# Token norms in two halves of 64 columns, and a new order in the last chunk of the state space stage

## The chip, the cores and the metric

The kernel runs on one core of a Trainium2 chip. The metric is the device time of one execution in microseconds (us), the median of the runs shown. A core has five engines that run their own instruction streams and wait for each other by semaphores: TensorE (PE, its weight loads are listed as PEld), VectorE (DVE), ScalarE (ACT), GpSimd (POOL) and SyncE (SP, which here only issues DMAs).

## The reference

Two transformer-like blocks over one sequence of 512 tokens with 1024 features, all in float32. Before and after each mixer stands an RMS norm over the features of a token:

```
def rms_norm(x, g):
    y = xf * lax.rsqrt(jnp.mean(xf * xf, axis=-1, keepdims=True) + EPS)
    return (y * g.astype(jnp.float32)).astype(x.dtype)

h = rms_norm(x, mix_pre_g) * (1.0 + sc1) + sh1
x = x + g1 * rms_norm(hybrid_mixer(h, ...), mix_post_g)      # attention and convolution
h = rms_norm(x, ffn_pre_g) * (1.0 + sc2) + sh2
x = x + g2 * rms_norm(swiglu_ffn(h, ...), ffn_post_g)
# second block
h = modulate(x, norm_g[0], shift, scale)
x = x + gate * mamba2_mixer(h, ...)                          # chunked state space, 4 chunks of 128 tokens
k, v = modulate(x, kv_norm_g, ...) @ kv_w
x = x + gate * sb_mixer(modulate(x, norm_g[1], ...), k, v, ...)   # stick-breaking attention
return rmsnorm(x, final_g)
```

At the end of the mamba2 mixer the output `y` is gated and normalised in 4 groups of 512 features, and then projected:

```
y = y.reshape(b, s, M_D_INNER) * jax.nn.silu(z)
yg = y.reshape(b, s, M_GROUPS, M_D_INNER // M_GROUPS)
yg = yg * lax.rsqrt(jnp.mean(yg * yg, axis=-1, keepdims=True) + EPS)
y = yg.reshape(b, s, M_D_INNER) * norm_g
return y @ out_w
```

## The kernel before

Features lie on the 128 partitions and tokens in the columns, so an activation is 8 tiles of 128x512. A float32 product is made from three passes: each operand is split into a high part and a rest (`whi` and `wlo` for weights, `hhi` and `hlo` for activations). Weights come in panels of 1 MB; ACT copies the high part of one (`split_hi`), DVE subtracts it (`split_lo`), and PE may use panel c only when `lo_split` has counted c + 1. There are two buffers, so a panel's split waits until the panel before its buffer has been used, and its DMA until the split of that one.

A norm over the features of a token is a sum over partitions. ACT squares a tile, and PE sums it with a matmul against ones (`token_sums`, one quarter of the tokens on each 32 partitions, so that all 512 sums lie in 128 columns). When all eight tiles are in, three steps follow each other, each on another engine: ACT takes the square root (`token_std`, 128x128), DVE the reciprocal in place (`token_rs`), and PE copies each quarter's row to all partitions by four float32 matmuls with a broadcast column of the identity as the weights (`spread`). Only then can DVE scale the tiles (L419 in a post-norm, L457 in a pre-norm, L2366 at the end), ACT makes the high part (L466), and PE starts the next product (L478). This chain is run seven times: once at the head of the kernel, twice after the attention (post-norm and the following pre-norm), twice after the FFN, once after the state space stage (its spread is the last thing before a block boundary, at which all engines meet) and once at the end.

`post_norm(..., late=(41, 54, sums, parts))` also places 13 small modulation products (`columns`, L382: 2 matmuls each, one column wide with 128x128 weights) on PE: `parts[0]` of them between the last sums and the first spread, `parts[1]` behind the first spread, `parts[2]` and `parts[3]` among the second sums, `parts[4]` ahead of the second spread, and `parts[5]` behind it.

In the state space stage every chunk has 8 batches of 4 heads. For each, ACT makes decays (L1726 to L1732), DVE masks them (`masked`, L1849 and L1854), and PE multiplies (L1578, L1581). The last chunk also gates the 4 groups on DVE (`gate_part`, L1379), squares them on ACT (`group_squares`, L1705), sums them on PE (`squares`, L1515), and takes root (`group_std`, L1716), reciprocal (`group_rs`, L1383), spread (`group_spread`, L1523) and the scaled low and high parts (`norm_lo`, L1388 and L1395; `hi_part`, L1407). The product with the output weights (`m_panel`, L1635) has eight panels; panel k of the first half needs group k. All orders are written out by hand: each engine runs its list in the order of the code, and nothing reorders it.

## Time and profile before

| | |
|---|---|
| time, median of 3 runs | 1412.69 us (1410.79 to 1412.97) |
| the profiled execution's own time | 1412.92 us |
| its span, first to last instruction | 1411.1 us |
| mean granted TensorE clock | 0.976 |
| busy: PE, DVE, ACT, POOL | 96%, 58%, 42%, 29% |

The busy shares are means over stages with different limits. The times below are in us from the start of the span, and all views are of this one execution. A matmul in float32 shows as two passes in the trace, each with its own weight load, so the 4 matmuls of a spread are 8 records.

### The profile page before, as it was taken

How to read it: one execution, taken by the hardware profiler on the slowest of the kernel's cores; microseconds unless marked ns; L12 is line 12 of the kernel's file. 1: busy time of each engine (PE TensorE's matmuls, PEld its weight loads, DVE VectorE, ACT ScalarE, POOL GpSimd, SP SyncE). 2: the span in 40 equal slices, each digit the busy share in tenths (PEclk: the TensorE clock that was granted, in tenths of full speed). 3: DMA queues.
4: the chain of work that ended last, by engine and by line, in shares of the span. 5: the costliest groups of instructions: out<-in, count | busy, mean ns of one | idle time of the engine just before them, and what ended most of it. 6: DMA issues, size and time to landing. Idle time of an engine off the chain costs nothing. (4 is left out here: it accounts for less than half of the span.)

```text
span 1411.1 us, 19533 instructions
## 1 busy us (share of the span) xinstructions
PE 1348.2 (96%) x7904; PEld 1072.8 (76%) x7904; DVE 823.5 (58%) x965; ACT 588.5 (42%) x849; POOL 407.2 (29%) x191
## 2 busy tenths in 40 slices
PE   5999999799999999999999999999998999999996
PEld 3778867578888888887788876767776899777775
DVE  2789974566555564433757656778733822566544
ACT  4323656332222232113444456787522422455441
POOL 0000000149887888998100000000000050232310
PEclk9999999889999999999799999999999999999998
DMA  9434071124545536543222243334132432111121
GB/s 382 156 136 150 31 268 61 60 90 178 186 171 223 189 128 235 209 178 149 93 91 89 92 131 93 113 119 143 60 111 91 156 121 90 60 60 34 57 90 60
DMA packets 41350, 181.12 MB, mean 128 GB/s; under 512 B 3392, under 2 KB 20160, under 8 KB 21312
## 3 DMA queue, kind: packets, MB, share of 16 engines
q1 hardware_dynamic: 40128, 171.73, 33.9%
q10 hardware_dynamic: 1152, 8.39, 1.7%
q8 instruction: 51, 0.84, 0.2%
q14 instruction: 19, 0.16, 0.0%
HBM read 173.75 MB, written 6.36 MB: 128 GB/s over the span
## 5 line engine op out<-in xcount | busy, mean ns | idle before, releaser
L193 DVE TENSOR_TENSOR wlo<-raw,whi 128x2048 fp32r<-128x2048 f32 x95 | 257.4, 2710 | 169.2 <-ACT whi L189 166.6
L200 POOL TENSOR_TENSOR ada_raw<-ada_raw,cs 128x2048 f32<-128x2048 f32 x36 | 142.6, 3962 | 498.6 <-DVE h2lo L451 451.0
L271 PE MATMUL ps<-hhi,whi 128*128 128x512 f32 x640 | 252.1, 394 | 2.3 <-PEq L563 0.8
L271 PE MATMUL ps<-hhi,wlo 128*128 128x512 f32 x640 | 249.4, 390 | 0.0
L271 PE MATMUL ps<-hlo,whi 128*128 128x512 f32 x640 | 249.1, 389 | 0.0
L189 ACT ACTIVATE whi<-raw 128x2048 fp32r<-128x2048 f32 x95 | 181.5, 1911 | 143.6 <-PE ps L1312 91.3
L209 POOL TENSOR_TENSOR ada_raw<-ada_raw 128x1024 f32<-128x1024 f32 x72 | 166.0, 2305 | 5.6
L271 PEld LDWEIGHTS ps<-hhi,whi 128*128 128x128 f32 x640 | 120.2, 188 | 28.6 <-issue 2.4
L271 PEld LDWEIGHTS ps<-hhi,wlo 128*128 128x128 f32 x640 | 120.1, 188 | 25.6
L271 PEld LDWEIGHTS ps<-hlo,whi 128*128 128x128 f32 x640 | 120.3, 188 | 24.3
L2041 POOL TENSOR_TENSOR x<-x,rest 128x256 f32<-128x256 f32 (+3 forms) x32 | 49.0, 1532 | 160.2 <-DVE rest L2340 160.2
L2340 DVE TENSOR_TENSOR_SCAN rest<-rest,zero 128x128 f32<-128x128 f32 (+3 forms) x64 | 59.0, 962 | 59.0 <-ACT rest L2257 59.0
L1262 ACT ACTIVATE fg<-ps 128x512 f32<-128x512 f32 x22 | 13.2, 599 | 174.4 <-PE ps L271 174.4
L739 DVE SCALAR_TENSOR_TENSOR cv<-u,vec,cv 128x512 f32<-128x512 f32 x120 | 81.9, 743 | 0.4
L1810 DVE SCALAR_TENSOR_TENSOR xbc<-ps,vec,xbc 128x511 f32 (+5 forms) x72 | 48.4, 741 | 41.9 <-ACT xbc L1666 41.8
L1277 DVE TENSOR_TENSOR fg<-ps,fg 128x512 f32<-128x512 f32 x22 | 15.2, 691 | 98.4 <-ACT fg L1262 98.4
L1312 PE MATMUL ps<-flo,whi 128*128 (+1 forms) x176 | 70.2, 399 | 0.0
L433 POOL TENSOR_TENSOR x<-x,y 128x512 f32<-128x512 f32 x4 | 5.1, 1270 | 225.0 <-DVE y L419 225.0
L1312 PE MATMUL ps<-fhi,whi 128*128 (+1 forms) x176 | 69.7, 396 | 0.0
L1312 PE MATMUL ps<-fhi,wlo 128*128 (+1 forms) x176 | 69.0, 392 | 0.0
L1503 PE MATMUL ps<-hhi,whi 128*128 128x512 f32 x128 | 55.3, 432 | 0.5 <-DVE wlo L193 0.5
L1503 PE MATMUL ps<-hlo,whi 128*128 128x512 f32 x128 | 50.3, 393 | 0.0
(374 smaller groups left out, 2781.1 us busy)
## 6 DMA issues: line engine op xcount, KB each, us to landing
raw<-panels SPq DMA_DIRECT2D x87, 1024.0 KB, 4.9
ada_raw<-ada SPq DMA_DIRECT2D x48, 1024.0 KB, 6.7
first<-ada SPq DMA_DIRECT2D x8, 1024.0 KB, 20.6
bc<-ac_rows SPq DMA_DIRECT2D x32, 256.0 KB, 3.7
raw<-panels ACTq DMA_DIRECT2D x8, 1024.0 KB, 5.0
x_kept<-x SPq DMA_DIRECT2D x2, 2048.0 KB, 9.7
x<-x_kept SPq DMA_DIRECT2D x2, 2048.0 KB, 7.7
x<-x_in SPq DMA_DIRECT2D x1, 2048.0 KB, 10.8
```

Of the source, the lines that this page charges most:

```text
L189: e.activation(whi[:, c % 2, :, :], raw[:, c % 2, :, :], ACT.Copy).then_inc(hi_split, 1)
L193: e.tensor_tensor(wlo[:, c % 2, :, :], raw[:, c % 2, :, :], whi[:, c % 2, :, :].bitcast(F32), ALU.subtract).then_inc(lo_split, 1)
L200: e.tensor_tensor(ada_raw[:, c % 2, :, :], ada_raw[:, c % 2, :, :], cs[:, which, :].unsqueeze(2).to_broadcast([P, KT, 256]), ALU.mult).the ...
L209: e.tensor_tensor((ada_acc[:, c % 2, :] if sums is None else sums).unsqueeze(1) if width == 1 else part, part, ada_raw[:, c % 2, width:2 * ...
L271: mm = e.matmul(ps[:, 2 * (qc % 2) + b, :], w[:, c % 2, 2 * k + b, :], src[part][:, k, :], **flags)
L739: dve.scalar_tensor_tensor(out=cv[:, j, :], in0=src, scalar=w, in1=cv[:, j, :], op0=ALU.mult, op1=ALU.add).then_inc(A["tap"], 1)
L1277: dve.tensor_tensor(fg[:, pair, :], ps[:, 2 * pair + 1, :], fg[:, pair, :], ALU.mult).then_inc(prod_ready, 1)
L1312: mm = pe.matmul(ps[:, b, :], w[:, c % 2, k2 * 8 + b, :], src[:, kt, :] if isinstance(i, int) else src[:, bass.ds(kt + i * 4, 1), :], star ...
L1503: mm = pe.matmul(ps[:, 2 * (qp % 2) + b, :], wt[:, cp % 2, 2 * kt + b, :], (hhi, hlo)[part][:, kt, :], start=(kt == 0 and j == 0), stop=(k ...
L1810: ins = dve.scalar_tensor_tensor(out=xbc[:, bass.ds(t, 1), s:S], in0=ps[:, 2 * pair + b, 0:S - s], scalar=vec[:, bass.ds(wc, 1)], in1=xbc[ ...
L2041: pool.tensor_tensor(sig[:, n % 3, :, 0:nk], sig[:, n % 3, :, 0:nk], rest[:, n % 2, :, S - nk + 1:S + 1], ALU.mult).then_inc(B["am"], 1)
L2340: scan = dve.tensor_tensor_scan(turned, turned, zero[:, 0:1].to_broadcast([P, nk]), 1.0, ALU.mult, ALU.add)
```

## The change

The square root, the reciprocal and the spread of the token norms work on 64 columns at a time (`TOKEN_HALVES`): two instructions on ACT, two on DVE, eight matmuls on PE instead of four. Each engine can start on a half when the engine ahead has finished that half; PE also waits for both square roots, since it overwrites the bank that they read. The norm of the groups in the state space stage is not split.

The small modulation products after the FFN move: `parts` goes from `[3, 3, 1, 1, 2, 3]` to `[4, 5, 1, 1, 2, 0]`.

In the last chunk of the state space stage the gate of group 0 comes behind the masks of batch 4 on DVE instead of ahead of them; on ACT the squares of group 3 come ahead of the high parts of group 2; the split of the fourth output panel (`cm + 3`) comes ahead of the scaled parts of group 3 on both engines. The coefficients of the two pre-norms of the last block are computed at the end of the block before.

```
         def token_std(act, no, s, bank):
             act.wait_ge(*no("ss_used", (s + 1) * KT))
-            act.activation(rsq[:], ps[:, bank, 0:P], ACT.Sqrt, bias=eps[:, 0:1],
-                           scale=1.0 / D).then_inc(nsem["std_ready"], 1)
+            for h in TOKEN_HALVES:
+                act.activation(rsq[:, h], ps[:, bank, h], ACT.Sqrt, bias=eps[:, 0:1],
+                               scale=1.0 / D).then_inc(nsem["std_ready"], 1)

         def token_rs(dve, no, s):
-            dve.wait_ge(*no("std_ready", s + 1))
-            dve.reciprocal(rsq[:], rsq[:]).then_inc(nsem["rs_ready"], 1)
+            for i, h in enumerate(TOKEN_HALVES):
+                dve.wait_ge(*no("std_ready", 2 * s + i + 1))
+                dve.reciprocal(rsq[:, h], rsq[:, h]).then_inc(nsem["rs_ready"], 1)

         def spread(pe, no, s, bank):
-            pe.wait_ge(*no("rs_ready", s + 1))
-            for b in range(TB):
-                mm = pe.matmul(ps[:, bank, b * P:(b + 1) * P], ident[:, 32 * b:32 * b + 1].to_broadcast([P, P]), rsq[:],
-                               start=True, stop=True)
+            pe.wait_ge(*no("std_ready", 2 * s + 2))
+            for i, h in enumerate(TOKEN_HALVES):
+                pe.wait_ge(*no("rs_ready", 2 * s + i + 1))
+                for b in range(TB):
+                    mm = pe.matmul(ps[:, bank, b * P + h.start:b * P + h.stop],
+                                   ident[:, 32 * b:32 * b + 1].to_broadcast([P, P]), rsq[:, h], start=True, stop=True)
             mm.then_inc(nsem["spread"], 1)
...
-                post2 = post_norm(..., late=(41, 54, sums, [3, 3, 1, 1, 2, 3]))
+                post2 = post_norm(..., late=(41, 54, sums, [4, 5, 1, 1, 2, 0]))
...                                                     # ACT, end of the state space stage
-                        hi_part(act, 2)
                         group_squares(3)
+                        hi_part(act, 2)
                         split_hi(act, cm + 2, 0)
                         group_std(3)
+                        split_hi(act, cm + 3, 0)
                         hi_part(act, 3)
                         act.activation(warm[:, 5:6], ones[:, 0:1], ACT.Sqrt)
-                        for k in range(1, MT // 2 - 1):
+                        for k in range(2, MT // 2 - 1):
...                                                     # DVE, last chunk
                                     if g < MG - 1 and not (c == TB - 1 and b == 1):
                                         masked(n + 2)
+                                        if c == TB - 1 and g == 1:
+                                            gate(0)
+                                            masked(n + 3)
...
-                                    if g < MG - 1:
+                                    if g in (0, 2):
                                         masked(c * NB + 2 * g + 3)
...
+                                    if g > 0:
+                                        gate(g)
...
                         norm_lo(dve, 2)
                         split_lo(dve, cm + 2, 0)
                         group_rs(dve, 3)
+                        split_lo(dve, cm + 3, 0)
                         norm_lo(dve, 3)
+                        norm_coefs(dve, v("kv_norm"), "kvsc", 1)
+                        norm_coefs(dve, v("norm2", KT, KT), "ssc", 2)
...                                                     # DVE, last block
-                    pre3["coefs"](dve)
-                    pre4["coefs"](dve)
                     pre3["dve"](dve)
```

On PE, behind the FFN: from the last sums of the post-norm (L316) over both spreads (`ps<-rsq`) to the first product of the next stage (L478). `macc` and `fg` hold the sums that the small modulation products read. First before, then after the change:

```order
L316 MATMUL ps<-y_place,consts 32x128 x12
L382 MATMUL ps<-consts,macc 128x1 x6
L336 MATMUL ps<-rsq,consts 128x128 x4
L382 MATMUL ps<-consts,macc 128x1 x6
L316 MATMUL ps<-y_place,consts 32x128 x12
L382 MATMUL ps<-consts,macc 128x1 x2
L316 MATMUL ps<-y_place,consts 32x128 x12
L382 MATMUL ps<-consts,macc 128x1 x2
L316 MATMUL ps<-y_place,consts 32x128 x8
L382 MATMUL ps<-consts,macc 128x1 x2
L382 MATMUL ps<-consts,fg 128x1 x2
L336 MATMUL ps<-rsq,consts 128x128 x4
```

```order
L317 MATMUL ps<-y_place,consts 32x128 x12
L387 MATMUL ps<-consts,macc 128x1 x8
L341 MATMUL ps<-rsq,consts 128x64 x8
L387 MATMUL ps<-consts,macc 128x1 x10
L317 MATMUL ps<-y_place,consts 32x128 x12
L387 MATMUL ps<-consts,fg 128x1 x2
L317 MATMUL ps<-y_place,consts 32x128 x12
L387 MATMUL ps<-consts,fg 128x1 x2
L317 MATMUL ps<-y_place,consts 32x128 x8
L387 MATMUL ps<-consts,fg 128x1 x4
L341 MATMUL ps<-rsq,consts 128x64 x8
L486 MATMUL ps<-hhi,whi 128x512
```

Two of the small matmuls moved ahead of the first spread and four more stand behind it; the six that stood behind the second spread are gone from there, and both spreads have twice the matmuls, each with weights of its own.

On ACT, in the last chunk, from the root of group 2 (`state<-ps`) to the split of the weight panels (`whi<-raw`). `ada_raw<-xbc` are the squares, `y2hi<-xbc` the high parts, `zb` the gate's silu. Before and after:

```order
L1716 ACTIVATE state<-ps,eps 128x128
L1698 ACT_TABLE_LOAD
L1698 ACTIVATE zb<-zb 128x1024 x2
L175 DMA raw<-panels 128x2048
L1407 ACTIVATE y2hi<-xbc 128x512 x4
L1705 ACTIVATE ada_raw<-xbc 128x512 x4
L189 ACTIVATE whi<-raw 128x2048
L1716 ACT_TABLE_LOAD
L1716 ACTIVATE state<-ps,eps 128x128
L1407 ACTIVATE y2hi<-xbc 128x512 x4
```

```order
L1706 ACTIVATE zb<-zb 128x1024 x2
L175 DMA raw<-panels 128x2048
L1713 ACTIVATE ada_raw<-xbc 128x512 x4
L1415 ACTIVATE y2hi<-xbc 128x512 x4
L189 ACTIVATE whi<-raw 128x2048
L1724 ACT_TABLE_LOAD
L1724 ACTIVATE state<-ps,eps 128x128
L189 ACTIVATE whi<-raw 128x2048
L1415 ACTIVATE y2hi<-xbc 128x512 x4
```

The four squares of group 3 now stand ahead of the four high parts of group 2, and the split of the third panel (`cm + 2`) stands where it stood, behind both; the split of the fourth panel moved ahead of the high parts of group 3.

On DVE, in the last chunk, from the skip terms of group 0 (`xbc<-xbc,vec,ps 128x128 x4`) over the masks (`dec`, `ce`) and the gate (`xbc<-xbc,x`) to the skip terms of group 1. Before and after:

```order
L1900 SCALAR_TENSOR_TENSOR xbc<-xbc,vec,ps 128x128 x4
L1849 TENSOR_TENSOR dec<-dec,cb 128x512
L1854 TENSOR_TENSOR ce<-ce,xbc 128x512
L1379 TENSOR_TENSOR xbc<-xbc,x 128x2048
L1849 TENSOR_TENSOR dec<-dec,cb 128x512
L1854 TENSOR_TENSOR ce<-ce,xbc 128x512
L1900 SCALAR_TENSOR_TENSOR xbc<-xbc,vec,ps 128x128 x4
```

```order
L1917 SCALAR_TENSOR_TENSOR xbc<-xbc,vec,ps 128x128 x4
L1858 TENSOR_TENSOR dec<-dec,cb 128x512
L1863 TENSOR_TENSOR ce<-ce,xbc 128x512
L1858 TENSOR_TENSOR dec<-dec,cb 128x512
L1863 TENSOR_TENSOR ce<-ce,xbc 128x512
L1387 TENSOR_TENSOR xbc<-xbc,x 128x2048
L1858 TENSOR_TENSOR dec<-dec,cb 128x512
L1863 TENSOR_TENSOR ce<-ce,xbc 128x512
L1917 SCALAR_TENSOR_TENSOR xbc<-xbc,vec,ps 128x128 x4
```

The gate of group 0 moved behind one more pair of masks, and the pair that followed the skip terms of group 1 now stands ahead of them.

## Rows read from the trace of the kernel before

**Rows 1.** The page: busy us (share) and instructions of each engine.

```profile
PE 1348.2 (96%) x7904; PEld 1072.8 (76%) x7904; DVE 823.5 (58%) x965; ACT 588.5 (42%) x849; POOL 407.2 (29%) x191
```

**Rows 2.** Timeline (start us, us, engine, line) of the norms after the attention.

```profile
268.50 0.37 ACT L324 ACTIVATE rsq<-ps,eps 128x128 f32<-128x128 f32 x1 [0.55 <-PE ps L316]
...
269.91 1.19 PEld L336 LDWEIGHTS ps<-rsq,consts 128*128 128x128 f32 x8 [1.74 <-DVE rsq L330]
...
282.69 1.78 PEld L336 LDWEIGHTS ps<-rsq,consts 128*128 128x128 f32 x8 [1.93 <-DVE rsq L330]
```

**Rows 3.** Two lines' own views: durations in ns (least/median/most).

```profile
L330 DVE RECIPROCAL rsq<-rsq x7: 952/953/953, 18.6 to 1399.4; 128x128 f32<-128x128 f32 x7
```

```profile
L1165 DVE RECIPROCAL rinv<-rsum x16: 148/154/165, 131.8 to 215.5; 128x2 f32<-128x2 f32 x16
```

**Rows 4.** Timeline of the norms after the FFN.

```profile
665.80 1.42 PEld L382 LDWEIGHTS ps<-consts,macc 128*128 128x128 f32 x12 [0.20 <-issue]
...
667.35 0.97 PEld L336 LDWEIGHTS ps<-rsq,consts 128*128 128x128 f32 x8
...
679.95 1.83 PEld L336 LDWEIGHTS ps<-rsq,consts 128*128 128x128 f32 x8
...
681.66 2.68 PEld L382 LDWEIGHTS ps<-consts,fg 128*128 128x128 f32 x12
...
682.89 1.38 ACT L466 ACTIVATE hhi<-y_place,mod 128x512 fp32r<-128x512 f32 x2 [4.10 <-DVE y_place L457]
...
684.28 0.77 PE L478 MATMUL ps<-hhi,whi 128*128 128x512 f32 x1
```

**Rows 5.** Stretches of PE: us, PE busy (passes), granted clock, DMA share, GB/s.

```profile
286.40:291.00 4.60, 4.55 (x11) 0.50 0.00 0
...
684.30:690.40 6.10, 6.10 (x15) 0.50 0.00 0
...
1085.60:1089.70 4.10, 1.48 (x19) 1.00 0.00 0
...
1092.00:1096.60 4.60, 4.59 (x11) 0.50 1.01 426
...
1400.40:1403.00 2.60, 2.06 (x8) 0.50 0.00 0
```

**Rows 6.** Timeline of the head and of the last block boundary.

```profile
19.57 0.97 PEld L336 LDWEIGHTS ps<-rsq,consts 128*128 128x128 f32 x8 [0.53 <-DVE rsq L330]
...
1090.15 0.24 DVE L443 SCALAR_TENSOR_TENSOR coef<-mod,vec 128x8 f32<-128x8 f32 x2 [1.54 <-PEq L1449]
```

**Rows 7.** Timeline of the last chunk, gate of group 0 to panel 0.

```profile
967.75 0.68 DVE L1849 TENSOR_TENSOR dec<-dec,cb 128x512 f32<-128x512 f32 x1
...
969.13 0.45 PE L1578 MATMUL ps<-dec,ada_raw 128*64 128x128 f32 x4 [0.94 <-DVE dec L1849]
...
982.75 0.47 PE L1635 MATMUL ps<-hhi,whi 128*128 128x512 f32 x1 [0.28 <-DVE hlo L1395]
```

**Rows 8.** Timeline of the last chunk behind the gate of group 3, by engine.

```profile
1007.29 2.17 ACT L1705 ACTIVATE ada_raw<-xbc 128x512 f32<-128x512 f32 x4
1009.37 1.89 ACT L189 ACTIVATE whi<-raw 128x2048 fp32r<-128x2048 f32 x1
...
1002.67 1.40 DVE L1388 SCALAR_TENSOR_TENSOR xbc<-xbc,vec,ps 128x512 f32<-128x512 f32 x2
...
1011.29 2.29 DVE L193 TENSOR_TENSOR wlo<-raw,whi 128x2048 fp32r<-128x2048 f32 x1 [3.19 <-ACT whi L189]
...
1008.01 0.23 PEld L1515 LDWEIGHTS ps<-ada_raw,consts 128*32 128x32 f32 x8 [3.29 <-issue]
...
1013.64 0.19 PEld L1635 LDWEIGHTS ps<-y2hi,whi 128*128 128x128 f32 x1 [0.40 <-DVE wlo L193]
...
1026.71 0.50 PE L1635 MATMUL ps<-y2hi,whi 128*128 128x512 f32 x1 [0.69 <-DVE wlo L193]
```

**Rows 9.** PE behind that wait: us, PE busy (passes), clock, DMA.

```profile
1008.00:1010.00 2.00, 1.96 (x32) 0.50 0.03 8
```

More of the change, by code:

```diff
@@ L342, in post_norm @@
             N = nsem
-            no = counting(bank_done=KT - 1, kept=KT, sq_ready=2 * KT, ss_used=2 * KT, std_ready=2, rs_ready=2, spread=2,
+            no = counting(bank_done=KT - 1, kept=KT, sq_ready=2 * KT, ss_used=2 * KT, std_ready=4, rs_ready=4, spread=2,
                           scaled=KT, x_new0=KT // 2, x_new1=KT // 2, coef_ready=1)
@@ L435, in post_norm, with norm_coefs @@
             return dict(pe=on_pe, act=on_act, coefs=coefs, mods=mods, dve=on_dve, pool=on_pool)
+        def norm_coefs(dve, gain, sc, slot, k0=0, k1=KT):
+            dve.scalar_tensor_tensor(out=coef[:, slot, k0:k1], in0=m(sc)[:, k0:k1], scalar=1.0, in1=gain[:, k0:k1],
+                                     op0=ALU.add, op1=ALU.mult).then_inc(nsem["coef_ready"], 1)
         def pre_norm(gain, sc, sh, thi, tlo, h0, rs, slot=1, parts=1):
@@ L442, in coefs @@
             def coefs(dve, k0=0, k1=KT):
-                dve.scalar_tensor_tensor(out=coef[:, slot, k0:k1], in0=m(sc)[:, k0:k1], scalar=1.0, in1=gain[:, k0:k1],
-                                         op0=ALU.add, op1=ALU.mult).then_inc(N["coef_ready"], 1)
+                norm_coefs(dve, gain, sc, slot, k0, k1)
             def on_dve(dve, k0=0, k1=KT):
@@ L558, in build @@
             x_landed = sem("x_landed")
-            x0 = counting(sq_ready=KT, ss_used=KT, std_ready=1, rs_ready=1, spread=1)
+            x0 = counting(sq_ready=KT, ss_used=KT, std_ready=2, rs_ready=2, spread=1)
             head = pre_norm(v("mix_pre"), "sc1", "sh1", hhi, hlo, h0, ps[:, 7, :], parts=4)
@@ L1226, in build @@
                 last = co + COUNT["ffn_out"] - 1
-                post2 = post_norm("ffn_post", "g2", y_place[:, 0:KT, :], y_place[:, 8:11, :], last, late=(41, 54, sums, [3, 3, 1, 1, 2, 3]))
+                post2 = post_norm("ffn_post", "g2", y_place[:, 0:KT, :], y_place[:, 8:11, :], last, late=(41, 54, sums, [4, 5, 1, 1, 2, 0]))
                 pre2 = pre_norm(v("norm2", 0, KT), "msc", "msh", hhi, hlo, y_place[:, 11:13, :],
@@ L1440, in build @@
                 xsq = dec[:, 0:2, :, :].rearrange("p a h t -> p a (h t)")
-                no = counting(bank_done=3, x_new1=KT, sq_ready=KT, ss_used=KT, std_ready=1, rs_ready=1, spread=1)
+                no = counting(bank_done=3, x_new1=KT, sq_ready=KT, ss_used=KT, std_ready=2, rs_ready=2, spread=1)
                 M = {k: sem("m_" + k) for k in ("cols", "cols_c", "wend0", "ends", "xdt", "xw", "bt", "btok",
@@ L1856, in masked, with gate @@
                                                   .to_broadcast([P, HB, P]), ALU.mult).then_inc(M["ce"], 1)
+                        def gate(g):
+                            dve.wait_ge(M["yskip"], 4 * (TB - 1) * MG + 4 * g + 4)
+                            dve.wait_ge(G["z"], 2 * g + 2)
+                            gate_part(dve, g)
                         for c in range(TB):
@@ L1954, in x_step @@
                                                      op1=ALU.add).then_inc(nsem["x_new1"], 1)
-                        for k in range(1, MT // 2 - 1):
+                        for k in range(2, MT // 2 - 1):
                             split_lo(dve, cm + k + 2, 0)
@@ L1987, in build @@
             pre4 = pre_norm(v("norm2", KT, KT), "ssc", "ssh", h2hi, h2lo, h0, ps[:, 7, :], slot=2)
-            fin = counting(bank_done=KT - 1, x_new1=KT, sq_ready=KT, ss_used=KT, std_ready=1, rs_ready=1, spread=1,
+            fin = counting(bank_done=KT - 1, x_new1=KT, sq_ready=KT, ss_used=KT, std_ready=2, rs_ready=2, spread=1,
                            out_ready=KT, out_stored=16 * KT)
```

6 lines of the change are left out of this document (2 added, 4 removed).

## The prediction, made before the changed kernel had run

> **What bounds the kernel now.** I read the page first: PE is busy for 96% of the span, so only what PE waits for, or what PE itself does more of, moves the time [rows 1]. The timelines of the places that the diff touches come next, since the mean hides them. Two kinds stand out. One is the token norm: root on ACT, reciprocal on DVE, spread on PE, with nothing else for PE to do. From the start of the root at 268.50 to the first weight load of the spread at 269.91 pass 1.41 us; the spread's loads then take 1.19 us there and 1.78 us at 282.69 [rows 2]. The other is the last chunk of the state space stage, where PE waits 0.94 us for a mask at 969.13 [rows 7], 3.29 us for the squares of group 3, and 0.69 us at 1026.71 for `wlo` [rows 8]. The split makes the 1.41 us shorter; the new order aims at the waits. So I ask what each pays.
>
> **What a half costs.** One reciprocal of 128 columns takes 953 ns, one of 2 columns 154 ns [rows 3]. On the line between them 64 columns take 0.54 us; I take that, bounds 0.48 (half) and 0.95. The root takes 0.37 us for 128 columns [rows 2]; no row has a shorter one of these, so I take 0.30, bounds 0.19 and 0.37. The first half then reaches PE after 0.30 + 0.54 and the two hand-overs of today (1.41 - 0.37 - 0.95 = 0.09), at 0.93 us instead of 1.41: 0.48 us earlier. The second half is ready at about 1.4 us, while PE still works on the first, so it costs no wait.
>
> PE pays for it. A spread goes from 4 matmuls to 8, from 8 passes to 16, each with its own load of 128x128 weights. What is a pass of 64 columns? The spread's 8 loads of 128 columns span 0.97 us at 667.35; the small modulation products, one column wide with the same weights, span 1.42 us for 12 at 665.80 [rows 4]. Without the last load's own 0.19 that is 0.111 and 0.112 us for a pass. At the half clock it is (1.83 - 0.33) / 7 = 0.214 and (2.68 - 0.33) / 11 = 0.214 [rows 4]. A pass of 128 columns and one of 1 column cost the same: the weight load sets it, and 64 columns lie between. So the eight more passes cost 0.89 us at the full clock (2.4 GHz), 1.71 us at half (1.2 GHz). Less the 0.48 won, a chain becomes **0.41 us longer at full, 1.23 us at half**. Bounds of one chain: -0.5 us if a pass of 64 columns cost half of one of 128, and +1.7 us if the start came no earlier.
>
> The Trainium skill ("TensorE: Matmul & The Clock Gate", section on the back-to-back issue gap) gives a gap by moving columns, N / 2.4 + 2.5 ns when warm, by which a pass of 64 would be the cheaper; its own LDWEIGHTS section counts the 128 columns of the weights instead. By the first rule the chains would give -2.7 us in place of the +5.7 below (rival C); the rows above bear out the second.
>
> **The seven chains, one by one.**
> Head: PE idles 0.53 us ahead of its spread [rows 6], so it can start early, but then issues 16 passes; +0.4 to +0.6. What follows (modulation, tiles, split of the first panel, next modulation) runs back to back over DVE, and PE goes on from it. Part of it lies at the half clock either way. +0.4, bounds 0 and +0.6.
> After the attention: the first spread starts at full and slows down in its last loads, 1.19 against 0.97 us [rows 2, 4]. With 16 passes more of them fall there: 0.41 and four to five passes 0.1 us slower, +0.8. The second is at half: +1.23.
> After the FFN, first: four small products now stand ahead, 16 passes or 1.78 us from 665.80, so the spread starts at 667.58 instead of 667.35; the early half is of no use. +0.23 and +0.89 = +1.12. Second: two products stand ahead as before and end when the reciprocal does, so nothing is won, +1.71. But six matmuls are gone behind it: today they keep PE until 684.28, while the high part is there at 682.89 + 0.72 (half of the pair's 1.38, rounded up) = 683.6. This gives 0.55 back: +1.16. The six matmuls put behind the first spread take 4 products more, 0.9 to 1.7 us, while PE waits for squares; covered. Uncovered it would be +1.
> Behind the state space stage: full clock until 1089.7 [rows 5], +0.41, and the two `coef` instructions at 1090.15 leave the path, 0.24 us for both and 0.21 to the next start [rows 6]: +0.2. At their new place DVE waits for panels.
> End: at the half clock from 1400.40 [rows 5]; the early half of a us has some passes at full. +0.8, bounds +0.4 and +1.23.
> Sum: 0.4 + 0.8 + 1.23 + 1.12 + 1.16 + 0.2 + 0.8 = **+5.7 us**.
>
> **The last chunk.** The mask of batch 4 waits behind the gate of group 0, until 967.75; with the gate behind it PE's 0.94 us at 969.13 goes. But that gate starts two steps of about 0.6 us (the mask rows, 0.68 each) later, and ACT squares group 0 only behind it, with the decays of the last two batches and the root of group 0 queued after the squares. Root, reciprocal and spread come later by about 1.3 us, where DVE had some 1 us in hand; panel 0, which already waits for `hlo` at 982.75 [rows 7], starts 0 to 0.3 us later. I take +0.15 for the edit: the stall moves, it does not go.
>
> The squares of group 3: their gate ends where DVE takes up the scaled parts, 1002.67. ACT can square from about 1003.0 to 1005.1 (2.17 us) instead of from 1007.29, and PE finds them ready: its 3.29 us wait goes. What is late next? The high parts of group 2 start at 1005.1 instead of 1003.4, so DVE's low parts end at 1009.7 instead of 1008.1, and the split of panel `cm + 2`, still behind both, starts at 1008.9 on ACT instead of 1009.37. DVE then splits at 1010.8 instead of 1011.29 [rows 8]. PE needs just this: at 1013.64 it starts the panel, released by `wlo`, after 0.40 us without a load [rows 8]. So PE, through with its old work at 1009.1, now waits there until 1013.2, for 4.1 us, and **wins only 0.45 us of 3.3**. The early split of `cm + 3` takes the 0.69 us at 1026.71, with the run-out of the last pass 0.9. Together -1.35.
>
> Today, behind the 3.29 us without work, PE runs at 0.50 [rows 9]; the work in that stretch is hidden, since PE meets `wlo` anyway. In the new order the wait is longer and what follows is not hidden: some 3 us of products at half the clock cost 1.5 us (bounds 0 and 2.2). Without the slow clock it is -1.2 for this part; with it, it is -1.35 + 0.15 + 1.5 = **+0.3 us**.
>
> **Sum.** 5.7 + 0.3 = 6.0, against the profiled execution's own 1412.92 us (span 1411.1 and 1.8 around it; it lies 0.23 above the median of 1412.69): **1418.7 us**, taken as a median 0.2 down from 1418.9. That is 0.4% slower.
>
> **Rivals.** What can be told from no change is about 0.2%, 2.8 us; so "faster" begins below 1409.9 and "slower" above 1415.5.
> A, the forecast: weight loads set the pass. 0.58; its own range 1416 to 1421.5.
> B, the order in the last chunk pays in full, since the split of `cm + 2` comes in time or the clock stays up: 3.3 and 0.9 and up to 0.4 us of the stretched squares, -4.6. For it: the waits are in the rows. Against it: ACT does the same work ahead of that split. 5.7 - 4.6 on 1412.9 is 1414. 0.16.
> C, the moving columns set the pass: a split spread is as long as before and starts 0.48 earlier. Then after the attention -1.0, after the FFN +0.2 and -0.55, boundary -0.7, end -0.5, head -0.2: -2.7, with +0.3 it is 1410.5. Against it: one column costs what 128 do. 0.07, about half of it with part of B, below 1409.9. The Trainium skill's rule of the issue gap (page above) would have it so.
> D, on the other side: the clock. The products behind the norms run at 0.50 for 4.60, 6.10 and 4.60 us [rows 5], half of this lost, 7.6 us, and the spreads there lose 0.8 each. If twice the loads keep PE at full through these stretches, 7.6 and some 2.5 us come back: 6.0 - 10.1, 1408.8. It decides from two of the three stretches. Against it: PE moves no more columns than before, and 36 small passes did not keep it up after the FFN. 0.05.
> E, the longer chains make the half-clock stretches longer: three to seven us more at half cost 1.5 to 3.5 us: 1420.2 to 1422.2. 0.14.
>
> **Range and chances.** 1412.5 to 1421.5: it leaves out C, D and about half of E. Slower: A's part above 1415.5 (0.55) and E, 0.69. Same: B, the rest of A and half of C, 0.22. Faster: D and the other half of C, 0.09.
>
> **What would show it.** Right: 16 loads of a spread spanning 1.85 us at full and 3.5 at half; two reciprocals of 0.54 us; the first load 0.93 us after the root's start (not after the FFN, where small products stand ahead); PE released by `wlo` at the start of panel `cm + 2` after about 4 us, and no wait before `cm + 3`; the first product after the FFN 2.3 us later from 665.80. Wrong: loads of 64 columns less than 0.1 us apart; panel `cm + 2` starting straight behind the squares of group 3; the granted clock at 1.00 in the pre-norms' first products.

## The result, and the profile after

The changed kernel takes 1423.67 us (median of 5, 1421.5 to 1425.69) beside 1412.97 us for the kernel before (median of 5, 1410.79 to 1414.84): a ratio of 1.0068, 95% interval 1.0053 to 1.0082. The ratio is not the quotient of the two medians: by it the loss is 9.6 us, by the medians 10.7. It is slower, as predicted, but by about 10 us and not by 6, and it lies above my range (1412.5 to 1421.5). Two later sets gave 1.0067 [1.0043, 1.0091] and 1.0076 [1.0059, 1.0093]. The profiled execution took 1425.69 us, with a span of 1423.5 us and a mean granted clock of 0.969 against 0.976.

The page of the changed kernel, busy us and instructions, answers to [rows 1]:

```profile
PE 1361.0 (96%) x7960; PEld 1086.6 (76%) x7960; DVE 821.6 (58%) x972; ACT 589.1 (41%) x856; POOL 405.2 (28%) x191
```

56 passes more (7 chains of 8), and PE is busy for 12.8 us more. By 0.112 and 0.213 us a pass (below) these are 6.3 us at the full clock and 11.9 if each were at the half clock, which few are: so more of the other work must have run slower too.

The timeline of the two norms after the attention, answers to [rows 2]:

```profile
272.24 0.52 ACT L326 ACTIVATE rsq<-ps,eps 128x64 f32<-128x64 f32 x2 [0.55 <-PE ps L317]
272.59 0.96 DVE L333 RECIPROCAL rsq<-rsq 128x64 f32<-128x64 f32 x2
...
273.26 2.58 PEld L341 LDWEIGHTS ps<-rsq,consts 128*128 128x128 f32 x16 [1.35 <-ACT rsq L326]
...
285.92 0.52 ACT L326 ACTIVATE rsq<-ps,eps 128x64 f32<-128x64 f32 x2 [0.78 <-PE ps L317]
...
286.93 3.49 PEld L341 LDWEIGHTS ps<-rsq,consts 128*128 128x128 f32 x16 [1.54 <-ACT rsq L326]
```

The first load now comes 1.02 us (272.24 to 273.26) after the root's start instead of 1.41. But sixteen loads take 2.58 and 3.49 us instead of 1.19 and 1.78. The two lines' own views, answering to [rows 3]:

```profile
L333 DVE RECIPROCAL rsq<-rsq x14: 494/524/554, 16.9 to 1410.9; 128x64 f32<-128x64 f32 x14
```

```profile
L326 ACT ACTIVATE rsq<-ps,eps x14: 297/308/313, 16.6 to 1410.3; 128x64 f32<-128x64 f32 x14
```

The timeline behind the FFN, answering to [rows 4], gives the price of a pass most plainly, since two kinds stand in a row:

```profile
672.26 1.86 PEld L387 LDWEIGHTS ps<-consts,macc 128*128 128x128 f32 x16 [0.20 <-issue]
...
674.04 1.87 PEld L341 LDWEIGHTS ps<-rsq,consts 128*128 128x128 f32 x16
...
687.48 3.53 PEld L341 LDWEIGHTS ps<-rsq,consts 128*128 128x128 f32 x16
```

Sixteen passes of one column took 1.86 us, sixteen of 64 columns 1.87 us. Less the last load's own 0.19 that is 0.112 us a pass either way, and (3.53 - 0.33) / 15 = 0.213 at the half clock.

Last, stretches of PE: us, PE, PEld, DVE, ACT and POOL busy, granted clock, DMA share, GB/s; they answer to [rows 5] and [rows 9]:

```profile
195.80:202.60 6.80, 6.80 (x36) 5.03 (x36) 3.05 (x7) 3.90 (x10) 0.00 (x0) 0.50 0.51 173
288.00:298.00 10.00, 8.31 (x27) 6.95 (x27) 7.08 (x11) 3.55 (x5) 0.00 (x0) 0.50 0.21 89
...
946.80:950.00 3.20, 3.20 (x18) 2.00 (x15) 2.81 (x9) 3.17 (x3) 0.00 (x0) 0.50 0.12 35
1022.70:1028.60 5.90, 5.86 (x15) 4.71 (x16) 3.14 (x2) 1.14 (x1) 0.00 (x0) 0.50 0.72 221
```

Two of these are new, 195.8 to 202.6 and 946.8 to 950.0, and they lie in the attention and in the state space stage, where the diff touches nothing. Two others are longer: PE is at 1.2 GHz until 298 (before: until 291.0, which is 294.7 with the 3.74 us that these norms start later), and behind the wait in the last chunk until 1028.6. Not all of this is lasting: r_after, a second profile of the same kernel, has the stretch in the attention stage, but not the one at 947, and the two others are no longer than before.

How late the changed kernel is, stage by stage. Each number is the median, over DVE's instructions that both traces have in that stretch of the kernel before (3 to 223 of them), of start now minus start before; the last is the difference of the spans:

| place (us of before) | profile of the result | 2nd profile (r_after) | 3rd profile (r2_after) | my sum up to there |
|---|---|---|---|---|
| behind the head (60 to 120) | -0.4 | +1.5 | +1.4 | +0.4 |
| attention stage, late (205 to 265) | +3.8 | +5.8 | +6.1 | +0.4 |
| behind the attention's norms (300 to 640) | +6.5 | +6.9 | +8.8 | +2.4 |
| behind the FFN's norms (700 to 930) | +8.0 | +8.0 | +10.3 | +4.7 |
| before the last chunk (951 to 965) | +9.6 | +8.0 | +11.9 | +4.7 |
| behind the last chunk (1045 to 1075) | +10.8 | +7.9 | +13.1 | +5.0 |
| last block (1110 to 1380) | +11.1 | +9.7 | +13.4 | +5.2 |
| end | +12.4 | +10.7 | +14.6 | +6.0 |

One line is out in all three: between 185 and 205 us the kernel loses 4.1 to 4.7 us where I had nothing. (An unchanged copy of the kernel before lies 1.8 us behind its first profile after the head, so differences of 2 us there are scatter.)

### The profile page after: what moved, and what is told of

It reads as the page before. It is cut to its first block and busy times, and to the rows that moved or that the text cites. A ratio compares the mean times of both kernels' runs of the same rounds, so it can differ in the third digit from the quotient of the medians.

```text
span 1423.5 us, 19666 instructions
## 1 busy us (share of the span) xinstructions
PE 1361.0 (96%) x7960; PEld 1086.6 (76%) x7960; DVE 821.6 (58%) x972; ACT 589.1 (41%) x856; POOL 405.2 (28%) x191
## 5 line engine op out<-in xcount | busy, mean ns | idle before, releaser
L1270 ACT ACTIVATE fg<-ps 128x512 f32<-128x512 f32 x22 | 13.2, 599 | 174.1 <-PE ps L271 174.1
```

## The experiments

Each kernel ran beside the kernel before on the same chip; ratios are to it. The sets differ by up to 4 us in what the kernel before takes (1412.97 to 1417.13), so I compare ratios, and a loss or gain in us is the ratio on that set's median. There is one profile of each kernel and set, of one execution.

### The halves, and the rest

e1_halves is the kernel before with the new `token_std`, `token_rs` and `spread` and nothing else; e2_rest is the changed kernel with these three as before.

```
-            for h in TOKEN_HALVES:                                    # e2_rest
-                act.activation(rsq[:, h], ps[:, bank, h], ACT.Sqrt, ...)
+            act.activation(rsq[:], ps[:, bank, 0:P], ACT.Sqrt, ...)
```

> The kernel before with the split token norms alone (root, reciprocal and spread in two halves of 64 columns), nothing else of the change. Theory 1, each pass of the spread is set by its weight load (0.111 us at the full clock, 0.214 at half): head +0.4 to +1, after the attention +0.9 and +1.2, after the FFN +0.7 and +1.7, boundary +0.4, end +1.2: +6 to +7.5 us. Rival C, moving columns set the pass: -3 us. Rival D, the added passes keep the clock up: -2 or less, and no stretch at 0.50 behind the norms.

> The changed kernel with the token norms whole again: only the order in the last chunk, the places of the small products and the coefficients. Theory 1: small products -0.3, coefficients -0.2, last chunk between -1.2 (clock stays up behind the new wait for wlo) and +1.5 (it falls to half for some 5 us): -1.7 to +1.0 us in all. If the order of the last chunk were worth what its waits show (rival B), -4.5 or less. If most of what the changed kernel lost beyond the forecast is in this part, +3 or more.

Measured: e1_halves 1422.61, ratio 1.0050 [1.0034, 1.0065], +7.1 us on 1414.68; e2_rest 1413.02, 0.9985 [0.9974, 0.9997], -2.1 us. The halves are the loss, and the other edits give a little. Their sum is 5, which is not the changed kernel's 9.6; the last two questions below take that up.

The chunk's order is seen alone in the timeline of e2_rest, answering to [rows 8]:

```profile
1010.98 2.29 DVE L193 TENSOR_TENSOR wlo<-raw,whi 128x2048 fp32r<-128x2048 f32 x1 [1.11 <-ACT whi L189]
...
1013.33 0.50 PE L1638 MATMUL ps<-y2hi,whi 128*128 128x512 f32 x1 [3.87 <-DVE wlo L193]
```

PE waits 3.87 us for `wlo` of `cm + 2`: the wait for the squares became a wait for the weights. The gate did no better: PE waits 0.43 and 1.03 us at the spread of group 0 and at panel 0, where it waited 0.94 us for the mask and 0.28 at panel 0.

### Which part of a half costs

e3_whole_spread keeps root and reciprocal in halves, but the spread waits for both and is four matmuls of 128 columns. e4_quarters has four pieces of 32 columns on all three engines.

```
-            for i, h in enumerate(TOKEN_HALVES):                      # e3_whole_spread
-                pe.wait_ge(*no("rs_ready", 2 * s + i + 1))
-                for b in range(TB): ...  rsq[:, h]
+            pe.wait_ge(*no("rs_ready", 2 * s + 2))
+            for b in range(TB): ...  rsq[:]
+        TOKEN_HALVES = tuple(slice(i, i + P // 4) for i in range(0, P, P // 4))    # e4_quarters
```

> As the first of this call, but PE waits for both halves and does the spread with 4 matmuls of 128 columns as before; root and reciprocal stay in two halves. Theory 1, the cost is the eight more weight loads: 0 us (-0.5 to +0.5), since two half reciprocals take as long as one. If the two more instructions on ACT and DVE or their semaphores cost it, +3 or more remain.

> Token norms in four pieces of 32 columns: 16 matmuls, 32 passes per spread. Theory 1: a chain is 24 passes longer (2.7 us at full, 5.1 at half) and starts about 0.65 us earlier: +2.0 at full, +4.5 at half, in the places above +18 to +23 us. Rival C (columns set the pass): the spread keeps its length and starts earlier, -4 us. A floor for each pass other than the weight load would lie between.

Measured: e3_whole_spread 1414.16, ratio 1.0004 [0.9992, 1.0015]; e4_quarters 1442.86, 1.0199 [1.0184, 1.0214], +28 us. With four matmuls the whole cost of the halves is gone, with sixteen it is four times as large. The 28 us are 5 more than the top of what I had expected; that profile has 99 us at the half clock in its span, the first one of before 69, and I had not counted on longer stretches. The timelines of the spread after the attention in e3_whole_spread, then in e4_quarters:

```profile
270.14 0.52 ACT L326 ACTIVATE rsq<-ps,eps 128x64 f32<-128x64 f32 x2 [0.55 <-PE ps L317]
...
271.50 0.97 PEld L339 LDWEIGHTS ps<-rsq,consts 128*128 128x128 f32 x8 [1.70 <-DVE rsq L333]
```

```profile
272.20 0.99 DVE L333 RECIPROCAL rsq<-rsq 128x32 f32<-128x32 f32 x4
...
272.76 5.16 PEld L341 LDWEIGHTS ps<-rsq,consts 128*128 128x128 f32 x32 [1.21 <-ACT rsq L326]
```

Four reciprocals of 32 columns take 0.99 us together, two of 64 took 0.96 and one of 128 took 0.95: cutting DVE's work costs almost nothing, cutting PE's costs a weight load for every piece.

### The clock in the norms

e6_warm is the kernel before with useless products of 128x512 on PE where it would wait in the norms; e7_warm_halves is the same with the halves. They compute nothing that is used.

```
+        def keep_warm(pe, n, bank):
+            for _ in range(n):
+                pe.matmul(ps[:, bank, :], ident_r, exact[:].rearrange("p a b -> p (a b)"), start=True, stop=True, ...)
...
+                keep_warm(pe, 4, 2)
                 spread(pe, no, 0, ORDER[0])
```

> The kernel before, with products of no use on PE (128x512, the constants, into a free bank, read by nobody) where it waits in and behind the token norms of both post-norms, of the boundary and of the end; whole norms, old order. If the half clock of these stretches is what such a norm costs beyond its chain: granted clock 1.00 from 268 us to 700 us and from 1085 us on, and -7 to -11 us. If the clock does not follow such work, 0 to +3 us, since some of them stand in the way.

> The same, with the token norms in two halves. Theory 1: a chain is then 0.41 us longer everywhere, 7 chains, one of them at the head partly hidden: +2.5 to +3 us against the one before it, in place of the 7.1 measured with the clock as it falls. If the halves cost 7 us here too, it is not the half clock that makes them dear.

Measured: e6_warm 1411.21, ratio 0.9971 [0.9954, 0.9987], -4.1 us on 1415.8; e7_warm_halves 1419.32, 1.0021 [1.0004, 1.0039], +3.0. Both are misses. e6_warm gained 4 us and not 7 to 11. Its clock did not stay up everywhere, and its profile has a half-clock stretch in the attention stage, ahead of all these products, behind which it is 3.1 us later; from there to its end it gains 5.5. And the halves cost as much here as with the clock as it falls: e7_warm_halves lies 7.1 us above e6_warm by the ratios (8.1 by the medians), and I had expected 2.5 to 3. I had written that the half clock would then not be what makes them dear; but the clock did not stay up, so the pair does not decide it. In the two profiles the distance grows by 0.9 us over the two norms after the attention and by 0.4 each at the boundary and at the end, which is the forecast for the full clock; but it grows by 2.3 us at the head, 1.3 in the attention stage and 5.3 over the norms after the FFN. At the head and in the attention stage no such product stands, and after the FFN they did not keep the clock up. Windows behind the FFN, e6_warm and then e7_warm_halves:

```profile
679.10:685.90 6.80, 6.80 (x25) 5.93 (x24) 6.19 (x9) 3.26 (x5) 0.00 (x0) 0.50 0.31 131
```

```profile
672.40:679.20 6.80, 6.80 (x40) 5.54 (x39) 5.23 (x9) 2.14 (x4) 3.27 (x3) 0.50 0.00 0
686.00:696.30 10.30, 10.30 (x38) 9.14 (x38) 7.38 (x11) 3.75 (x6) 0.00 (x0) 0.50 0.20 84
```

So the pair gives the cost of single chains at the full clock, but not that of seven. The norm after the attention in e6_warm, then in e7_warm_halves:

```profile
282.54 0.37 ACT L324 ACTIVATE rsq<-ps,eps 128x128 f32<-128x128 f32 x1 [0.55 <-PE ps L316]
...
283.95 0.97 PEld L336 LDWEIGHTS ps<-rsq,consts 128*128 128x128 f32 x8 [0.78 <-DVE rsq L330]
```

```profile
286.63 0.52 ACT L326 ACTIVATE rsq<-ps,eps 128x64 f32<-128x64 f32 x2 [0.55 <-PE ps L317]
...
287.65 1.86 PEld L341 LDWEIGHTS ps<-rsq,consts 128*128 128x128 f32 x16 [0.40 <-issue]
```

From the root's start to the end of the last load it is 1.41 + 0.97 = 2.38 us whole and 1.02 + 1.86 = 2.88 us in halves: +0.50 at the full clock, where I had 0.41. At the half clock the kernel before has 1.41 + 1.78 = 3.19 us, from this root to the spread at 282.69 in [rows 2]:

```profile
281.28 0.37 ACT L324 ACTIVATE rsq<-ps,eps 128x128 f32<-128x128 f32 x1 [0.78 <-PE ps L316]
```

The changed kernel has 1.01 + 3.49 = 4.50 us: +1.31, where I had 1.23.

### A better order for the last chunk

e5_split2_first has whole norms and brings the split of `cm + 2` ahead of the squares of group 3 on ACT and of the scaled parts of group 2 on DVE; the gate of group 0 stays where it was, and PE does the spread of group 3 one step later.

```
                         for p in range(turned, MT // 2):
                             silu_z(p)
+                        split_hi(act, cm + 2, 0)
                         group_squares(3)
...
+                        split_lo(dve, cm + 2, 0)
                         norm_lo(dve, 2)
-                        split_lo(dve, cm + 2, 0)
```

> Whole token norms; small products and coefficients as changed; in the last chunk the squares of group 3 first and panel cm + 3 early as changed, but the gate of group 0 as before, and the split of panel cm + 2 ahead of the squares on ACT and ahead of the scaled parts of group 2 on DVE, spread of group 3 one step later. My account of the order (PE's wait for the squares only turned into a wait for the split of cm + 2): both waits go, -4.5 in the chunk and -0.5 outside, -5 us. If the split of cm + 2 was not what held PE, -1 to -2 as with the order of the changed kernel.

Measured: 1410.17, ratio 0.9952 [0.9934, 0.9970], -6.8 us. Its windows view, in the columns of the other windows views above:

```profile
1000.00:1020.00 20.00, 20.00 (x124) 16.41 (x123) 15.74 (x16) 14.21 (x18) 0.00 (x0) 1.00 0.30 106
```

PE is busy in all of the 20 us and stays at 2.4 GHz. By the stage offsets the chunk takes 5.7 us less than before. So what rival B spoke of is there to be had, once the split comes first. The later spread goes with it and was not tried alone; the gate matters little, for PE's waits at it are 0.94 and 0.28 us here and 0.43 and 1.03 in e2_rest.

### Is it the parts together?

r_after is the changed kernel again. e8_halves_parts has the halves, the moved small products and the coefficients; e9_halves_order has the halves and the last chunk's order. r_before is the kernel before against itself. Each edit is the piece of the diff in the section on the change. The expectation of r_after was written with e5 to e7:

> The changed kernel again, unaltered, beside the others of this call. The halves alone lost 7.1 us (interval 4.8 to 9.2) and the rest won 2.1 (0.4 to 3.7), together 5; the changed kernel lost 9.6 when measured by itself. If the parts add up, it loses 3.5 to 7 here; if they work against each other, 9 or more again.

> The kernel before, once more, unchanged. Two things are asked. Its time against itself says how far two equal kernels come apart here: 0 expected, within 0.15%. And its profile says whether the half-clock stretch at about 195 to 205 us, which five of the ten profiles so far have (the changed kernel's twice, two kernels with whole norms among them) and the first profile of before has not, comes to this kernel too. Theory 'chance': it does in about half of its executions, so there it may be present or absent, and the stage between 185 and 265 us then lies 3.4 to 4.3 us later or does not. Theory 'the change causes it': never in this kernel.

> The halves, the moved small products behind the FFN and the moved coefficients, with the last chunk in its order of before. The halves alone cost 7.1 us and the rest alone gave 1.5 to 2 us, which makes 5 to 5.6 us, but the changed kernel lies 9.0 to 9.6 us above before. Theory 'they add up': the six small products moved away from behind the second spread give 0.5 us and the coefficients 0.4 us, so +6.2 us (range +4.5 to +7.5). Theory 'the small products cost with the halves': ten of their matmuls and a spread of 16 passes stand ahead of the second sums, all at half the clock, and the second root comes late: +9 us or more. Theory 'chance' (the attention stage and what a median of five to eleven executions leaves): as the first, and the difference of the changed kernel is in no part of it.

> The halves and the new order of the last chunk (gate of group 0, squares of group 3, split of the fourth panel), with the small products and the coefficients as before. Theory 'they add up': +7.1 for the halves and about -1 for the order (with whole norms the rest together gave 2 us, of which the coefficients and the small products have about 0.9), so +6 us (range +4.5 to +7.5). Theory 'the order costs with the halves': in the profile of the changed kernel PE waits 3.9 us for the split of the third panel and then runs at half the clock for 6.8 us, where the same order with whole norms had 3.4 us of it: +8.5 us or more, and a half-clock stretch of 6.8 us behind that wait.

Measured: r_after 1424.71, ratio 1.0067 [1.0043, 1.0091]; r_before 1416.14, 1.0000 [0.9984, 1.0017]; e8_halves_parts 1425.91, 1.0052 [1.0036, 1.0069]; e9_halves_order 1424.02, 1.0051 [1.0035, 1.0066]. By ratio the halves with either other part cost +7.4 and +7.2 us on 1417.13, what they cost alone. Both are where "they add up" put them. The intervals reach to 9.8 and 9.4 us, so the times alone do not rule the two "costs with the halves" theories out; the profile of e9_halves_order does not have what the second one asks for, since it is at half the clock for 3.4 us behind the wait for `wlo` and not for 6.8. The changed kernel is again at more than the halves alone, +9.5 us.

What these traces had was a pattern. At about 194 us PE waits a second time for the modulation rows (`ada_raw<-ada`). In the kernel before, then in the changed one:

```profile
190.89 1.07 PE L229 MATMUL ps<-ada_raw,cs 128*32 128x256 f32 x16 [0.54 <-DMA ada_raw<-ada]
...
194.06 1.07 PE L229 MATMUL ps<-ada_raw,cs 128*32 128x256 f32 x16 [0.96 <-DMA ada_raw<-ada]
...
195.65 0.61 PE L244 MATMUL ps<-quad,ada_acc 128*128 128x1 f32 x4
```

```profile
190.76 1.07 PE L229 MATMUL ps<-ada_raw,cs 128*32 128x256 f32 x16 [0.80 <-DMA ada_raw<-ada]
...
194.86 1.09 PE L229 MATMUL ps<-ada_raw,cs 128*32 128x256 f32 x16 [1.88 <-DMA ada_raw<-ada]
...
196.93 1.01 PE L244 MATMUL ps<-quad,ada_acc 128*128 128x1 f32 x4
```

The same four products take 0.61 us in the one and 1.01 in the other: behind the longer wait PE runs at 0.50. The second wait and the stretch, in all profiles without products put there:

| | second wait, us | half clock at 194 to 205 us |
|---|---|---|
| before, r_before, e2, e3 | 0.96, 1.44, 1.42, 1.31 | none |
| e1, r_halves, e9, e4 | 1.56, 1.57, 1.37, 1.15 | none |
| changed kernel, three profiles | 1.88, 2.02, 2.42 | 6.8 us each |
| e8, e7 (halves) | 1.68, 2.05 | 6.8 us each |
| e5, e6, e10 (whole norms) | 2.32, 2.08, 2.09 | 6.8, 3.4, 6.8 us |

Whole norms have it too, so it is not the halves that make it. e6_warm differs from the kernel before only in products that come later than this stage, so it is not the change alone either, though the two profiles of before have no stretch here; but the changed kernel had it in three profiles of three.

### The wait in the attention stage

e11_fill is the changed kernel with nine useless products of 256 columns ahead of that second wait. r_halves is e1_halves again, r2_after the changed kernel again, on the same chip.

```
                         def rows(a):
+                            if a == 15:
+                                pe.wait_ge(rows_kept, a)
+                                for _ in range(9):
+                                    pe.matmul(ps[:, MODB, 256:512], ident_r, exact[...][:, 0:256], start=True, stop=True, ...)
                             pe.wait_ge(ada_landed[a % 2], ...)
```

> The changed kernel once more, unchanged, beside the halves alone and beside the kernel before on the same chip. Two sets so far gave +9.5 and +9.6 us by the ratio (intervals from about +6 to +13), the halves alone +7.1, and the halves with either other part +7.3 and +7.4. Theory 'they add up': +7 to +8 here. Theory 'the parts cost together what none costs alone': +9.5 or more, and at least 2 us above the halves alone on this chip.

> The halves alone once more (five runs were few): +7 us, range +5.5 to +8.5. By my seven chains they cost 5.7 us less what the moved small products and coefficients save, so +6.7; by the stage offsets of the profiles so far they cost +0.3 at the head, +1.7 after the attention, +2.3 after the FFN, +1.0 at the boundary and +1.3 at the end, 6.6 in all, and a stretch at the half clock that comes by chance in the attention stage is on top where it comes.

> The changed kernel with nine useless products of 256 columns (about 1 us) on PE in the attention stage, between the seventh and eighth of its modulation row loads, where PE then waits for the DMA of ada_raw. In 14 profiles so far that wait is 0.96 to 1.56 us in the seven without a half-clock stretch at 195 to 205 us and 1.68 to 2.32 us in the seven with it, and the stage behind it is 3.4 to 4.3 us longer in those. Theory 'the stretch comes from the length of this wait': the wait becomes about 1 us shorter, the stretch is gone from every execution, and the median falls by half of 4 us, -1.5 to -2.5 against the changed kernel on this chip; the profile has no half clock there. Theory 'the wait and the stretch only go together by chance': no change, or +0.3 where the DMA was in time, and the stretch in half of the executions.

Measured: r2_after 1427.18, ratio 1.0076 [1.0059, 1.0093]; r_halves 1422.74, 1.0052 [1.0033, 1.0072]; e11_fill 1422.43, 1.0048 [1.0031, 1.0065]. The fill takes 4.75 us off the changed kernel's median (4.0 by the ratios), and all six runs with it lie below all six without. That is more than the 1.5 to 2.5 that I had written, where I had counted on the stretch in half of the executions. In its timeline the wait is 0.47 us, and the windows view grants the full clock behind it:

```profile
194.36 1.31 PE L920 MATMUL ps<-exact 128*128 128x256 f32 x9
...
196.14 1.07 PE L229 MATMUL ps<-ada_raw,cs 128*32 128x256 f32 x16 [0.47 <-DMA ada_raw<-ada]
```

```profile
196.00:204.00 8.00, 7.86 (x88) 5.34 (x88) 6.09 (x11) 5.32 (x12) 0.00 (x0) 1.00 0.75 242
```

By the stage offsets the piece from 185 to 205 us now costs 1.0 us instead of 4.7, and the changed kernel lies 6.8 us above before by the ratio: near where my sum had put it (+6.0). In the profiles r2_after ends 7.6 us behind e11_fill, since it also has the short stretch at 949 (1.6) and the long one in the last chunk (1.2); r_after, which has neither, ends 3.7 behind, of which the attention stage gives 3.4. As to r2_after, +10.8 us and 3.4 above the halves alone is on the side of "the parts cost together", with the two intervals overlapping.

### The best kernel

e10_warm_split2 joins e5_split2_first and e6_warm; e12_warm_fill adds the fill to it.

> Whole norms, the moved small products and coefficients, the last chunk with the split of the third panel (cm + 2) ahead of the squares of group 3, and useless 128x512 products on PE while it would wait in the norms. The two parts lie in different stages and gave -5.6 and -4.6 us against before, so about -10 us (range -7.5 to -12), and a mean granted clock of 0.99. If what the earlier split gave were the clock alone (the products keep it up in the norms only, not there), the sum is the same; if both were worth what they gave only by chance, -3 to -6.

> The best kernel so far (whole norms, split of the third panel ahead of the squares of group 3, useless products in the norm waits; -12.6 us in its medians, -13.2 by the ratio) with the same nine products in the attention stage. Its profile had the half-clock stretch there (wait 2.09 us). By the first theory it gains 1.5 to 4 us more, -14 to -17 against before; by the second nothing. If the wait stays above 1.7 us in spite of the products, nothing either.

Measured: e10_warm_split2 1404.49, ratio 0.9907 [0.9886, 0.9928], -13.2 us; e12_warm_fill 1406.92, 0.9928 [0.9910, 0.9947], -10.2 us. The first beats both kernels, by what its parts gave and a little over. The second is a miss: the stretch is gone from its profile (wait 0.75 us), but the time did not fall. A later row load came late instead (the last line), yet the piece from 185 to 205 us still costs 2.8 us and not the 4.6 of e10_warm_split2:

```profile
195.08 1.07 PE L229 MATMUL ps<-ada_raw,cs 128*32 128x256 f32 x16 [0.75 <-DMA ada_raw<-ada]
...
203.50 1.07 PE L229 MATMUL ps<-ada_raw,cs 128*32 128x256 f32 x16 [1.38 <-DMA ada_raw<-ada]
```

What this profile loses again it loses elsewhere. Over the norms after the FFN it falls back by 3.8 us against e10_warm_split2, with stretches of 10.2 and 6.8 us at the half clock where that one has a single one of 6.8, and by 1.6 behind a short stretch at 940:

```profile
667.00:677.20 10.20, 10.20 (x52) 8.45 (x51) 8.32 (x13) 3.18 (x6) 5.11 (x4) 0.50 0.01 2
684.00:690.80 6.80, 5.97 (x16) 4.26 (x15) 6.33 (x9) 3.39 (x5) 0.00 (x0) 0.50 0.01 2
```

So what the fill gives in time is shown for the changed kernel alone.

## Why the prediction was too low

**The price of a pass: right.** Weight loads set it: 0.112 us at 1 and at 64 columns, 0.213 at the half clock, as read from [rows 4]. The gap by moving columns that the Trainium skill gives ("TensorE: Matmul & The Clock Gate", Back-to-back issue gap) would be, as an estimate by its rule, 29 ns for 64 columns; this case's rows, at 112 ns, do not agree. But the Trainium skill gives that rule, in the same section, for a single matmul apart, and says that in a stream of weight loads and matmuls both set the spacing; so the Trainium skill does not speak for rival C as I had it. Its section on LDWEIGHTS, which counts the columns of the weights, goes with this case's rows. e3_whole_spread and e4_quarters show it in the time: 0, +7 and +28 us for 4, 8 and 16 matmuls. Rival C is out, and so is D: behind the norms after the attention and after the FFN the clock is at 0.50 for 23.9 and 20.5 us, before for 20.5 each.

**The halves on ACT and DVE: right.** Reciprocal 0.52 us (0.54), root 0.31 (0.30), first load after 1.02 us instead of 0.93; a chain is 0.50 and 1.31 us longer where I had 0.41 and 1.23. That adds some 0.6 us over seven chains. The first product after the FFN comes 20.6 us behind the first small product instead of 18.5: 2.15 us later, 2.3 forecast. (The working says there that six matmuls more stand behind the first spread; it is four, and the time it gives them is that of four.)

**The last chunk: right in its steps.** The wait for batch 4 is gone and has moved, as forecast: PE waits 0.43 and 1.03 us later on instead of 0.94 and 0.28, +0.24 where I had +0.15. The squares are ready (PE's own row of the wait for them had 2.90 us; the 3.29 in [rows 8] is the gap of its weight loads), and the timeline of the changed kernel, answering to [rows 8], has PE waiting for `wlo` for 3.88 us (4.1 forecast), with nothing ahead of `cm + 3`:

```profile
1018.47 1.89 ACT L189 ACTIVATE whi<-raw 128x2048 fp32r<-128x2048 f32 x1
...
1020.39 2.29 DVE L193 TENSOR_TENSOR wlo<-raw,whi 128x2048 fp32r<-128x2048 f32 x1 [1.11 <-ACT whi L189]
...
1021.94 1.90 ACT L189 ACTIVATE whi<-raw 128x2048 fp32r<-128x2048 f32 x1
...
1022.74 0.80 PE L1643 MATMUL ps<-y2hi,whi 128*128 128x512 f32 x1 [3.88 <-DVE wlo L193]
```

The size moves with the clock: with 3.4 us at half behind it (e2_rest, r_after) the chunk costs +0.1 and -0.1 us, with 6.8 us (the two other profiles) +1.2 each; I had +0.3. In e8_halves_parts, which has the old order, 6.8 us at half make it +1.2 as well, so that us is the clock's and not the order's. Rival B is out for this order; e5_split2_first shows that it fell to the place of one split, with the spread that goes with it.

**The step that failed is the sum itself**, "5.7 + 0.3 = 6.0, against the profiled execution's own 1412.92": it gave nothing to the stages that the diff does not touch. Of the 12.4 us in the profile of the result, 4.1 lie between 185 and 205 us, behind a DMA wait that grew from 0.96 to 1.88 us, and 1.6 in the short stretch at 946.8. Without these two it is 6.7; without the piece from 185 to 205 us (and the 1.6 in the third) the two other profiles are at +6.4 and +8.3. e11_fill is the test: with the wait shortened, the changed kernel is at +6.8. The mechanism was in my working only for the norms (rival E, +1.5 to +3.5), and so the range ended at 1421.5. I had also one execution of before to read, with 0.976; 103 later ones of it have medians of 1415.7 us and 0.975. The 24 of them at 0.972 or less take 1418.9 us in the mean, the 44 at 0.976 or more 1413.9: 5 us that go with the clock, over four chips, in a kernel that nobody changed. The 18 of the changed kernel have a mean of 0.971.

**What stays open.** Why the second row load lands late in every profile of the changed kernel and of e8_halves_parts, but in none of three with halves alone or halves and order. It is not issued late: SyncE issues it 2.1 us behind the load before it in all of them. The transfer itself takes longer, 6.8 to 7.5 us from issue to landing in the eight profiles with the stretch and 5.8 to 6.5 in the eight without (6.9 in the profile of the result, 5.8 in the first of before). Moving the small products and the coefficients is common to those (and to e5 and e10, which have it too, but also to e2, which has not), and e6 and e7 have it without them. The load is the same and its stage is untouched; what makes the transfer slower was not tried. With it stays open how much of the 3 us between the changed kernel and the halves alone is a lasting cost: the intervals of the two ratios on one chip overlap.

## What to carry to other kernels

Cut a chain into halves only on the engines whose time goes with the columns; where a matmul's weights are as wide as its moving data or wider, a half costs what the whole did (in these runs: float32 passes with weights of 128 columns). When work is brought ahead of a wait, follow everything that then stands in front of the next release: here the place of one split of weights decided between nothing and 5.7 us in the chunk. And a sum over the edited places is only as good as the quiet of the others: look through the whole trace for waits that lie close to where the clock fell elsewhere, and widen the range by what one such stretch costs.

## What the runs showed of the hardware

A wait of PE for a DMA of 0.96 to 1.57 us in a stage of small products left the granted clock at 1.00 in eight profiles; one of 1.68 to 2.42 us was followed by 3.4 or 6.8 us at 0.50 in eight, and the piece from 185 to 205 us then took 3.1 to 4.8 us longer than in the first profile of before, against 0 to 0.9 in the seven others of the first eight. About a us of waiting more thus went with some four in time; in the changed kernel nine useless products in the wait took them away. And useless work on PE around the norms, which raised the mean granted clock from 0.976 to 0.991 in the profiles and cut the time at the half clock from 69 to 25 us, gave 4 us: much less than the 22 us that half of the 44 would be. The rest of that time PE was waiting, or others set the pace; the two were not told apart.
